# Experts 0 to 6 of a mixture layer: their rows come back through DRAM and four indirect gathers, not by selection products

## The reference

```python
def swiglu(x, w13, w2):
    a, g = jnp.split(x @ w13, 2, axis=-1)
    return (jax.nn.silu(a) * g) @ w2

def moe_ffn(x, router_w, router_b, w13, w2):
    logits = (x @ router_w).astype(jnp.float32) + router_b.astype(jnp.float32)
    top_v, top_i = lax.top_k(logits, TOP_K)
    wts = jax.nn.softmax(top_v, axis=-1)
    gate = jnp.einsum('bsk,bske->bse', wts, jax.nn.one_hot(top_i, N_EXPERTS, dtype=jnp.float32)).astype(x.dtype)
    y = jnp.zeros_like(x)
    for e in range(N_EXPERTS):
        y = y + gate[..., e:e + 1] * swiglu(x, w13[e], w2[e])
    return y
...
        x = layer_norm(ALPHA * x + y, ln_g[l, 1], ln_b[l, 1])
```

## Time and profile before

| | |
|---|---|
| median of 3 runs | 2275.1 us (2274.92 to 2275.48) |
| span of the profiled execution | 2273.5 us |
| PE busy | 2252.9 us (99%) |
| DVE busy | 1753.8 us (77%) |
| ACT busy | 1372.5 us (60%) |
| POOL busy | 75.7 us (3%) |
| data read from DRAM | 577.16 MB, 254 GB/s over the span |
| expert stage (first weights' DMA to the last row back) | about 1280 to 2263 us |

### The profile page before, as it was taken

The page is one execution under the profiler, slowest core; times in us unless marked ns, Lnnn a source line. Parts: engine busy times, 40 slices in busy tenths (PEclk is TensorE's granted clock), DMA queues, the critical chain, the costliest instruction groups (busy, mean ns, idle before and its releaser), DMA issues.

```text
span 2273.5 us, 30626 instructions
## 1 busy us (share of the span) xinstructions
PE 2252.9 (99%) x12406; PEld 1936.7 (85%) x12406; DVE 1753.8 (77%) x2264; ACT 1372.5 (60%) x1797; POOL 75.7 (3%) x95
## 2 busy tenths in 40 slices
PE   9999999999999999999999999999999999999997
PEld 6998888998888999888899888888888888888886
DVE  6876546977554588555678899989998999989997
ACT  5654444655443454444445587777777777777775
POOL 2200001300000001000100000000000000000000
PEclk9999999999999999999999999999999999999999
DMA  7445454545553535554425699999999999999995
GB/s 261 163 187 193 175 202 148 178 170 213 185 185 130 182 130 215 207 189 167 167 101 185 249 353 373 369 354 360 371 365 358 352 365 377 364 347 364 376 363 216
DMA packets 94308, 580.29 MB, mean 255 GB/s; under 512 B 21792, under 2 KB 23120, under 8 KB 25040
## 3 DMA queue, kind: packets, MB, share of 16 engines
q1 hardware_dynamic: 80496, 568.74, 66.7%
q10 hardware_dynamic: 13664, 9.52, 1.5%
HBM read 577.16 MB, written 1.06 MB: 254 GB/s over the span
## 4 chain that ended last, share of the span: by engine, by line
PE 96%; DVE 2%; issue 1%; ACT 0%; POOL 0%; DMA 0%; ACTq 0%; DVEq 0%
PE bank L469 28%; PE bank L471 28%; PE bank L470 28%; PE bank L466 9%; PE bank L699 2%; PE bank L745 1%; PE bank L499 1%; DVE wl L1584 1%; POOL SM L2387 0%; PE bank L793 0%; DMA LNB<-in_ln 0%; ACT wh L1150 0%; DVE BIAS L1930 0%; ACT HH L1163 0%; DVE XL L2229 0%
## 5 line engine op out<-in xcount | busy, mean ns | idle before, releaser
L1584 DVE TENSOR_TENSOR wl<-raw,wh 128x1024 fp32r<-128x1024 f32 x698 | 819.6, 1222 | 222.5 <-ACT wh L1150 219.6
L1150 ACT ACTIVATE wh<-raw 128x1024 fp32r<-128x1024 f32 x704 | 704.7, 1054 | 311.4 <-PE bank L471 273.4
L469 PE MATMUL bank<-wh,GH 128*128 128x512 f32 x896 | 352.1, 393 | 0.7 <-DVE wl L1584 0.7
L471 PE MATMUL bank<-wh,GL 128*128 128x512 f32 x896 | 349.3, 390 | 0.0
L470 PE MATMUL bank<-wl,GH 128*128 128x512 f32 x896 | 348.9, 389 | 0.0
L1584 DVE TENSOR_TENSOR wl<-spare,wh 128x1024 fp32r<-128x1024 f32 x264 | 309.6, 1220 | 25.7 <-ACT wh L1150 24.4
L1150 ACT ACTIVATE wh<-spare 128x1024 fp32r<-128x1024 f32 x264 | 264.4, 1054 | 63.9 <-PE bank L471 63.8
L469 PE MATMUL bank<-HH,wh 128*128 128x256 f32 x832 | 239.6, 288 | 0.0
L470 PE MATMUL bank<-HL,wh 128*128 128x256 f32 x832 | 235.3, 283 | 0.0
L471 PE MATMUL bank<-HH,wl 128*128 128x256 f32 x832 | 235.2, 283 | 0.0
L469 PE MATMUL bank<-wh,HH 128*128 128x512 f32 (+1 forms) x600 | 224.9, 375 | 2.2 <-DVE wl L1584 2.0
(11 more groups left out here) (277 smaller groups left out, 3471.4 us busy)
## 6 DMA issues: line engine op xcount, KB each, us to landing
raw<-in_ws SPq DMA_DIRECT2D x352, 1024.0 KB, 5.9
spare<-in_ws SPq DMA_DIRECT2D x132, 1024.0 KB, 6.6
more<-in_ws SPq DMA_DIRECT2D x48, 1024.0 KB, 4.8
once<-in_ws SPq DMA_DIRECT2D x4, 1024.0 KB, 11.5
REL<-in_relb ACTq DMA_DIRECT2D x4, 768.0 KB, 12.4
LNB<-in_ln ACTq DMA_DIRECT2D x3, 1024.0 KB, 5.9
LNB<-in_ln ACTq DMA_DIRECT2D x4, 512.0 KB, 4.7
raw<-in_ws SPq DMA_DIRECT2D x2, 816.0 KB, 4.6
```

The source lines that it names most:

```text
L469: T.q.matmul(o, l[0], r[0], start=start, stop=False)
L471: return T.q.matmul(o, l[1], r[0], start=False, stop=stop)
L1150: A.q.activation(sets[c % NSET][0][:, half * i:half * i + half], raws[stream.place[n]][:, half * i:half * i + half], ACT.Copy).then_inc(*h ...
L1584: V.q.tensor_tensor(wl[:, half * i:half * i + half], raw[:, half * i:half * i + half], wh[:, half * i:half * i + half].bitcast(f32), ALU.s ...
```

## The change

For experts 0 to 6 the way back is no longer a product.

- ACT copies the two result banks as plain float32 into `Y[e % 2]` (`a_down_copy`); DVE's `YL` for them goes. POOL writes `Y` (512 KB) to a scratch tensor `parts` in DRAM, 128 rows of 4 KB per expert (`g_parts`).
- `v_rows`, in expert 0 after chunk 2, makes for each token the two row numbers in `parts` (`ROWS`); `v_choice_weights`, after chunk 3, the two weights. A token whose second expert is 7 has weight 0 there.
- Once expert 7's last hidden product is finished, POOL issues four indirect gathers of 128 rows of 4 KB (2 tiles x 2 choices) into `CHOICE`. `v_add_choice` adds weight x row to `X` in four DVE steps of 1024 columns, one after each of the splits of slots j = 6, 7, 8, 9 of expert 7's down projection.
- `t_scatter`, `v_scatter`, `SEL` and its transposes stay for expert 7 and for the second page alone. Expert 7's last way back is as before.

```diff
+        def a_down_copy(e):
+
+            if e >= 2:
+                A.wait_ge(*part_out[e % 2].at(e - 2))
+            for h in range(2):
+                a_copy(Y[e % 2][:, 512 * h:512 * h + 512], ("dn", ("e", e), 0, h), 512)
...
+                if e < 7:
+                    a_down_copy(e)
+                    continue
...
                 t_most()
             for e in range(8 * page, 8 * page + 8):
                 between, later = [], []
-                if e % 8:
+                if page and e % 8:
                     between += [lambda t=t: t_scatter(e - 1, t) for t in range(2)]
-                if e % 2 == 0:
+                if page and e % 2 == 0:
                     between += [lambda: t_turn_sel(e // 2)]
-                elif e % 8 < 7:
+                elif e == 6:
+                    between += [lambda: t_turn_sel(3, (1,))]
+                elif e % 2 and e % 8 < 7:
                     later = t_gather(e // 2 + 1)
...
             v_tokens(1)
-            for e in range(2):
-                v_choose(e, select)
             v_lo(expert_slot(0) + 1)
...
+        def v_rows():
...
+            V.q.tensor_scalar(ROWS[:, :], PICK[:, 64:68], -1.0, 0.0, ALU.add, ALU.max).then_inc(*picked.mark())
...
+        def v_add_choice(i):
+
+            c, t = i // 2, i % 2
+            V.wait_ge(*choice_in[i].at())
+            V.wait_ge(*(added.at(t, 0) if c else scaled.at("dn", 3)))
+            V.wait_ge(*choice_weight.at())
+            V.q.scalar_tensor_tensor(XV[:, t, :], CHOICE[i][:, :], PICK[:, 68 + i:69 + i], XV[:, t, :], ALU.mult,
+                                     ALU.add).then_inc(*added.mark(t, c))
...
-                if e % 8:
+                if page and e % 8:
                     between += [lambda t=t, e=e: v_scatter(e - 1, t) for t in range(2)]
                 if e == 0:
-                    between += [lambda: None, v_gates_end]
+                    between += [lambda: None, v_gates_end, v_rows, v_choice_weights]
...
                     if j == 0:
                         turn()
-                for h in range(2):
+                    if e == 7 and 6 <= j < 10:
+                        v_add_choice(j - 6)
+                for h in range(2) if e > 6 else ():
...
+        def g_parts():
+
+            for e in range(7):
+                for h in range(2):
+                    G.wait_ge(*out("dn", ("e", e), 0, h))
+                G.q.dma_start(parts[128 * e:128 * e + 128, :], Y[e % 2][:, :]).then_inc(*part_out[e % 2].mark(e))
+            G.wait_ge(*picked.at())
+            for x in (5, 6):
+                G.wait_ge(*part_out[x % 2].at(x))
+            G.wait_ge(*full("gu", ("e", 7), 6, 0))
+            for i in range(4):
+                G.q.indirect_dma_start(
+                    out=CHOICE[i][:, :], out_offset=None, in_=parts,
+                    in_offset=bass.IndirectOffsetOnAxis(ap=ROWS[:, i:i + 1], axis=0),
+                    bounds_check=7 * 128 - 1, oob_is_err=False).then_inc(*choice_in[i].mark())
```

More of the change, by code:

```diff
@@ L100 @@
 C_OWN = 1128
-NCONST = 1136
+C_ROWS, C_KEPT = 1136, 1144
+NCONST = 1152
 def constants():
@@ L118, in constants @@
     c[:, C_ROW:C_ROW + 128] = q
+    c[:, C_ROWS:C_ROWS + 8] = 128.0 * np.arange(8)[None, :]
+    c[:, C_KEPT:C_KEPT + 7] = 1.0
     for h in range(4):
@@ L342, in program @@
         GH, GL = at("GH", 16384, 2048, f32r), at("GL", 18432, 2048, f32r)
+        Y = [at(f"Y{i}", 14336 + 1024 * i, 1024) for i in range(2)]
+        CHOICE = [at(f"CHOICE{i}", 16384 + 1024 * i, 1024) for i in range(4)]
         SEL, SELR, SELT = at("SEL", 20480, 512), at("SELR", 20992, 512, f32r), at("SELT", 21504, 512, f32r)
@@ L455, in program @@
             signal(n) for n in ("router_split", "gap", "gap_exp", "gate_done", "chosen", "tokens_in"))
+        picked, choice_weight, added = signal("picked"), signal("choice_weight"), signal("added")
+        part_out = [signal(f"part{i}_out", 16) for i in range(2)]
+        choice_in = [signal(f"choice{i}_in", 16) for i in range(4)]
         flag, select, selr, yhi, ydone = (signal(n) for n in ("flag", "select", "selr", "yhi", "ydone"))
@@ L1058, in t_gather, with t_turn_sel @@
             return [lambda c2=c2, v=v: move(c2, v) for c2 in range(4) for v in range(2)]
-        def t_turn_sel(p):
+        def t_turn_sel(p, own=(0, 1)):
             room = groups.take(T, "sel", p)
-            for i in range(2):
+            for i in own:
                 for t in range(2):
@@ L1504, in a_gather, with a_last_select @@
             return [lambda c2=c2, v=v: move(c2, v) for c2 in range(4) for v in range(2)]
+        def a_last_select():
+            A.wait_ge(*full("sel", 3))
+            A.q.activation(SELT[:, 256:512], groups.bank("sel", 3)[:, 256:512],
+                           ACT.Copy).then_inc(*groups.empty("sel", 3))
+        def a_down_copy(e):
[3 more added lines that the diff above has]
+                a_copy(Y[e % 2][:, 512 * h:512 * h + 512], ("dn", ("e", e), 0, h), 512)
         def a_experts(page):
@@ L1513, in a_experts @@
                 between, later = [], []
-                if e % 8:
+                if page and e % 8:
                     between += [lambda: None] * 2
-                if e % 2 == 0:
+                if page and e % 2 == 0:
                     between += [lambda: a_copy(SELT[:, :], ("sel", e // 2), 512)]
-                elif e % 8 < 7:
+                elif e == 6:
+                    between += [a_last_select]
+                elif e % 2 and e % 8 < 7:
                     later = a_gather(e // 2 + 1)
@@ L2280, in v_choose @@
             V.wait_ge(*out("pos"))
-            if p:
-                V.wait_ge(*(out("ga", p - 1, 1, 3) if mark is selr else out("sel", p - 1)))
+            if p and mark is selr:
+                V.wait_ge(*out("ga", p - 1, 1, 3))
+            elif p >= 4:
+                V.wait_ge(*out("sel", p - 1))
             for t in range(2):
@@ new lines, in v_choice_weights @@
+        def v_choice_weights():
+            kept, rows, gates, own = (PICK[:, 16 * i:16 * i + 16].rearrange("p (t n) -> p t n", t=2) for i in range(4))
+            for t in range(2):
+                V.wait_ge(*gate_done.at(t))
+            V.wait_ge(*picked.at())
+            V.q.tensor_tensor(own, rows, PICK[:, 64:66][:, :, None].to_broadcast([128, 2, 8]), ALU.is_equal)
+            V.q.tensor_tensor(PICK[:, 32:48], GW, PICK[:, 0:16], ALU.mult).then_inc(*step.mark())
+            V.wait_ge(*step.now())
+            V.q.tensor_reduce(PICK[:, 70:72], gates, AX.X, ALU.add)
+            V.q.tensor_tensor(own, own, gates, ALU.mult).then_inc(*step.mark())
+            V.wait_ge(*step.now())
+            V.q.tensor_reduce(PICK[:, 68:70], own, AX.X, ALU.add).then_inc(*step.mark())
+            V.wait_ge(*step.now())
+            V.q.tensor_tensor(PICK[:, 70:72], PICK[:, 70:72], PICK[:, 68:70],
+                              ALU.subtract).then_inc(*choice_weight.mark())
@@ L2307, in v_experts @@
                 between = []
-                if e % 8:
+                if page and e % 8:
                     between += [lambda t=t, e=e: v_scatter(e - 1, t) for t in range(2)]
                 if e == 0:
-                    between += [lambda: None, v_gates_end]
+                    between += [lambda: None, v_gates_end, v_rows, v_choice_weights]
                 if e % 2 and e % 8 < 7:
-                    between += [lambda x=x, m=m: v_choose(x, m) for m in (selr, select) for x in (e + 1, e + 2)]
+                    between += [lambda x=x, m=m: v_choose(x, m) for m in (selr, select) for x in (e + 1, e + 2)
+                                if page or m is selr or x == 7]
                 turn = v_swiglu(expert_slot(e), E_CHUNKS, 1, ("e", e), EV, between)
```

27 lines of the change are left out of this document (25 added, 2 removed).

## The result

The changed kernel took 2261.22 us (median of 4, 2260.55 to 2262.25) against 2275.12 us before; the ratio is 0.9939 with a 95% interval of 0.9927 to 0.9951. It is faster by 13.9 us, 0.61%. The forecast was 2261.0 us.

The account below looks back on a forecast made before the run. PE, busy 99% of the span, was taken as the bound. 2273.5 - 15.0 + 0.4 + 0.5 = 2259.4 us of span, with the median 1.6 us above it: 2261.0 us, 0.6% faster; range 2258 to 2268 us.

Parts of the forecast that it names:

- (a): PE, expert stage: the removed products with `SELT`, 14 places of 0.91 us, 12.7 us off.
- (b): PE, chunk ends of experts 0, 2, 4 and 6: removed transposes of `SEL`, 0.43 us a place, 1.5 us off.
- (c): Ahead of the stage: DVE's four `SEL` pieces go, PE is ready sooner at 1297.21; 0.8 us off (0 to 0.8).
- (d): Experts 0 to 6: DVE's adds and `YL` splits and three ACT `SELT` copies go; PE waits for none, 0.
- (e): Expert 0: DVE's added `v_rows` and `v_choice_weights` steps make a split late; 0.4 us on (0 to 2.6).
- (f): Expert 7's down projection: DVE's four adds make the last splits late; PE ends 0.5 us later (0 to 1.0).
- (h): Transfers: writes and gathers fit beside the loads, loads up to 1.5 us late covered by 2.9 us of spare; cost 0.
- rival 1: Expert 7: gathers' 5 us of transfers and POOL's work coincide with late splits; costs 3 to 5 us; chance 0.12.
- (g): Expert 7: gathered rows, 4.7 us each, 18.8 us for four, land before DVE's adds; nothing waits.
- Rival 3: Expert 7: slow gathers one after another, DVE waits at adds; costs from 7.8 us per gather on; chance 0.06.
- rival 2: Expert stage: transfers are the bound at 372 GB/s; 2270.5 us, no change; chance 0.07.
- (i): Outside the span: starting POOL's DMA queue may cost time; taken as 0 (0 to 2 us).

Follow-up runs that it names:

- pe_back: Changed kernel with 56 products of 512 columns put back on PE alone, at chunk ends 1 and 2 of experts 1 to 7; 2273.26 us.
- again: The changed kernel run again without an edit, as the measure for others beside it; 2261.17 us.
- no_gathers: Changed kernel without the four indirect gathers; the adds stay and take rows already on the chip; 2260.38 us.
- again_2: The changed kernel without an edit, run once more on a later occasion; 2261.78 us.
- serial_gathers: Changed kernel with each gather issued only when the one before has landed; 2265.07 us.
- gathers_twice: Changed kernel with four more gathers of the same rows, into an unused region, ahead of the four; 2265.97 us.
- late_both: Changed kernel with adds after splits j = 6 and 8 and two after the last split, third and fourth gather held until the last load's issue; 2260.82, 2260.01 us.
- held_gathers: Changed kernel with the four gathers held back until the split of slot 33 of expert 7 has ended; 2263.75 us.

## Why the prediction was right, step by step

**(a), the products: right to a tenth.** 14 places of 0.91 us; the leads in the table rise by 0.9 each, and pe_back gives 12.7 us. The listed durations summed would have given 23 us.

**(b), the transposes: 1.4 us, where 1.5 was forecast.** Experts 2 and 4 gave 0.41 each. In expert 6 the two that stay were moved by the change from chunk 2 to chunk 0, and the lead there rises by only 0.16 us in all (0.42 off, 0.25 on), where I had put 0.2. Together that is 1.0 us. Expert 0's 0.43 lie in the stretch of the next term.

**(c), the start: right in size, hidden in the profiled execution.** From the first gather product to the turn after chunk 1 the kernel before needs 1314.15 - 1286.18 = 27.97 us and again 1313.07 - 1286.37 = 26.70: 1.27 us, that is 0.43 for expert 0's transposes and 0.84, PE's whole wait at 1297.21. In the first profiled execution 0.95 us of it went to the lower clock (27.65 us), and all that lay ahead of the stage was 0.3 us later. The forecast's test (that wait gone) holds: in this execution PE waits for nothing from there to the tail.

**(d): right.** pe_back shows it.

**(e), DVE's steps in expert 0: wrong, 0 where 0.4 us was forecast.** They took less than was said, the eight 1.2 us (1.5 forecast) and the six 0.9 (1.1 forecast):

```profile
1327.77 0.17 DVE L2338 SCALAR_TENSOR_TENSOR PICK<-SM,CST 128x16 f32<-128x16 f32 x1
...
1328.98 0.69 DVE L1803 TENSOR_TENSOR TU<-TT,bank 128x512 f32<-128x512 f32 x1
1329.58 4.62 DVE L1617 TENSOR_TENSOR wl<-spare,wh 128x1024 fp32r<-128x1024 f32 x4
```

The split starts at 1329.58, its first half is ready at about 1330.8, and PE, which starts the chunk at 1325.88, wants it 24 matmuls later, at 1331.3. So PE doesn't wait. The step that failed is the comparison of 1.5 us added with a spare of 1.3: the added steps came to 1.2 us, and DVE entered them at 1327.77, where it had reached this place at 1328.33 before. It was as much ahead at the step after chunk 1 already (1316.03 against 1316.59); that (c) had let it start sooner fits, but was not tested. So the split was 0.65 us late (1329.58 against 1328.93), not 1.5.

**(f), the adds: right alone (0.4 us by no_gathers, 0.5 forecast), too small in company.** The step that failed is in (h), where loads up to 1.5 us late behind the gathers were held to be covered by the splits' 2.9 us of spare. The lateness was sized about right (ACT waited up to 1.7 us for one load, up to 1.9 in again_2), but the same 2.9 us had been spent in (f). Each of the two was counted against the whole spare. Together they cost 0.8 to 1.6 us, where (f) and (h) had 0.5. That is rival 1's mechanism at about a third of its price.

**(g), the rows in time: the answer right, the working wrong.** I took 4.7 us for a gather, from a plain load, and four one after another. A gather does take that, but only with no loads beside it (the fourth of serial_gathers); beside them one alone took 8.3 to 9.2 us, and the four of the changed kernel 8.6 to 16.9. The first landed some 12 us before its add, the fourth at about 2228.6, some 10 us before its own at 2238.73. Rival 3's threshold, 7.8 us per gather one after another, was right: in serial_gathers the third and fourth add wait for rows, and that kernel is 3.3 us slower than the changed one. What saved the change is that the four overlap, which the working had not assumed; that the answer held is luck in this respect.

**(h), the transfers: right against rival 2, wrong for the gathers, as said under (f).** The stage's windows of 24 us carried up to 402 GB/s, up to the tail ACT waited for PE and not for loads, and the writes cost nothing. The Trainium skill, page DMA: Bandwidth & Descriptors, section Where 436 GB/s comes from, sets about 358 GB/s for loads from DRAM. The kernel moved 369 GB/s on the mean from 1290 to 2250 us, so here, with one core at work, it doesn't bind.

**(i): right, nothing outside the span.** Each execution of the changed kernel lies 1.2 to 1.4 us above its span (the profiled one 2262.25 against 2261.0), as each of the kernel before that ran beside again does (1.2 to 1.4). The 1.6 us that the forecast added to its span was 0.3 too much: it set a median against the span of one execution.

The sum by what was measured: 12.7 + 1.4 (with expert 0's transposes and the move in expert 6) + 0.8 off, 0 and 0.8 to 1.6 on, 13.3 to 14.1 us off; measured 13.9, 13.7 and 13.0 us between medians. The forecast had 14.1. The large term, 12.7 of 14.9 us, was right for the reason given. That the forecast hit to 0.2 us is partly luck: (e) was 0.4 too dear, the tail 0.3 to 1.1 too cheap.

## What to carry to other kernels

Where one engine is full and all others wait for it, an instruction removed from it is worth its distance of starts. What the change lightens elsewhere is worth something only where the full engine waits for it, as at the start of the stage (0.8 us here). A wait of the full engine can cost more than itself: after 2.5 and 3.1 us of it the clock was at half for a while (1.5 and 2.8 us more). Spare time behind such an engine is one account: add up everything that draws on it at the same place, extra steps of a feeder and a burst of transfers together, before calling any of them covered. A gather should be issued early enough for its landing beside the loads, and a burst of several can be split around the last loads and its last steps put where the feeder is idle anyway; both together took the tail back to 37.6 us here.

## What the runs showed of the hardware

An indirect gather of 128 rows of 4 KB, issued by POOL beside loads at full rate, landed after 8.3 to 9.2 us alone (serial_gathers), after 8.6 to 16.9 with four in flight (median 12.7, the changed kernel), and after 22.6 in the median behind four others (gathers_twice). With the loads over it took 4.7 us. A plain write of 512 KB by POOL took 8.4 us and loads of 1 MB about 7. POOL itself was occupied for 1.0 to 1.1 us per indirect gather in the changed kernel, up to 2.0 in others (gathers_twice, late_both), and 0.5 us per write. DVE's busy stream of splits showed no slowing from any of them: a pair of splits is 2.34 to 2.38 us with gathers being issued or not.

The granted clock fell to the lower level (0.50 from 1288 to 1290 us) at the start of the stage in one execution and not in another of the same kernel (1.00), at 1.1 us to the first expert product in this place. It also fell after PE's waits of 2.5 us (serial_gathers) and 3.1 us (gathers_twice) in the tail, to 0.50, with 0.43 us from start to start of a product of 512 columns instead of 0.23, and stayed at 1.00 in held_gathers, where the longest wait was 1.5 us.
